# One-hot rows of the expert spread: compare and multiply in one instruction per token

## The reference

```
s = einsum('nhid,hikd->nhik', q, sub_keys)
s_top, i_top = top_k(s, 16)
cand = s_top[:, :, 0, :, None] + s_top[:, :, 1, None, :]
cand_idx = i_top[:, :, 0, :, None] * 128 + i_top[:, :, 1, None, :]
best, pos = top_k(cand.reshape(n, 8, 256), 16)
idx = take_along_axis(cand_idx.reshape(n, 8, -1), pos)
w = softmax(best)
act = gelu(einsum('nhkd,nd->nhk', take(u_tab, idx), hb))
out = einsum('nhk,nhkd->nd', w * act, take(v_tab, idx))
```

## Time and profile before

| | |
|---|---|
| median of 3 runs | 2853.62 us (2851.63 to 2854.61) |
| profiled execution | 2853.46 us, span 2851.7 us |
| mean granted TensorE clock | 0.988 |
| TensorE busy | 2768.9 us (97%) |
| VectorE busy | 1917.7 us (67%) |
| ScalarE busy | 1030.1 us (36%) |
| GpSimd busy | 608.7 us (21%) |

### The profile page before, as it was taken

One profiled execution on the slowest core, in us unless ns is written; L12 is line 12 of the kernel. 1 busy time (PEld: TensorE's weight loads), 2 busy tenths in 40 slices (PEclk: granted clock), 3 DMA queues, 4 the chain that ended last, 5 costly groups with the idle time before them and its releaser, 6 DMA issues. The chain is left out here.

```text
span 2851.7 us, 42463 instructions
## 1 busy us (share of the span) xinstructions
PE 2768.9 (97%) x15946; PEld 2469.1 (87%) x15946; DVE 1917.7 (67%) x3204; ACT 1030.1 (36%) x1502; POOL 608.7 (21%) x432
## 2 busy tenths in 40 slices
PE   8999999999999999999999999999999999899998
PEld 7886778898787898999998999999998777688877
DVE  7666553444445589899966677877777654588843
ACT  6433342223333343344443333333334433322222
POOL 4332000000000166565553322222220000100000
PEclk9999999999999999999999999999999999999999
DMA  3111222201332367888899999999996211232332
GB/s 128 49 56 46 76 94 82 82 29 67 96 96 97 95 216 241 274 288 283 274 298 345 372 318 343 340 342 343 341 341 223 67 45 61 66 100 92 94 89 76
DMA packets 271094, 496.68 MB, mean 174 GB/s; under 512 B 119249, under 2 KB 176721, under 8 KB 270178
## 3 DMA queue, kind: packets, MB, share of 16 engines
q1 hardware_dynamic: 215650, 335.26, 36.4%
q0 software_dynamic: 36864, 134.23, 12.7%
q10 hardware_dynamic: 18432, 25.17, 2.4%
HBM read 442.17 MB, written 52.43 MB: 173 GB/s over the span
## 5 line engine op out<-in xcount | busy, mean ns | idle before, releaser
L283 PE MATMUL banks<-experts_third,weights_high 128*128 128x384 f32 x1024 | 346.0, 338 | 1.0 <-DVE experts_third L2313 1.0
L284 PE MATMUL banks<-experts_third,weights_high 128*128 128x384 f32 x1024 | 345.9, 338 | 0.0
L285 PE MATMUL banks<-experts_third,weights_low 128*128 128x384 f32 x1024 | 345.9, 338 | 0.0
L2086 ACT ACTIVATE weights_high<-weights_raw 128x1024 fp32r<-128x1024 f32 x128 | 135.9, 1062 | 346.7 <-PE banks L285 346.7
L283 PE MATMUL banks<-hn_high,weights_high 128*128 128x264 f32 (+1 forms) x736 | 254.7, 346 | 4.2 <-DVEq L2672 1.7
L2127 POOL TENSOR_TENSOR weights_low<-weights_raw,weights_high 128x1024 fp32r<-128x1024 f32 x63 | 151.2, 2401 | 488.8 <-ACT weights_high L2029 488.7
L283 PE MATMUL banks<-hb_high,weights_high 128*128 128x384 f32 x688 | 240.9, 350 | 7.6 <-DVE weights_low L2292 5.3
L284 PE MATMUL banks<-hn_low,weights_high 128*128 128x264 f32 (+1 forms) x736 | 246.6, 335 | 0.0
L285 PE MATMUL banks<-hn_high,weights_low 128*128 128x264 f32 (+1 forms) x736 | 246.4, 335 | 0.0
L285 PE MATMUL banks<-hb_high,weights_low 128*128 128x384 f32 x688 | 234.1, 340 | 0.0
L284 PE MATMUL banks<-hb_low,weights_high 128*128 128x384 f32 x688 | 234.0, 340 | 0.0
(11 more groups left out here) (574 smaller groups left out, 7083.2 us busy)
## 6 DMA issues: line engine op xcount, KB each, us to landing
weights_raw<-in_u SPq DMA_DIRECT2D x128, 512.0 KB, 6.9
weights_raw<-in_v SPq DMA_DIRECT2D x128, 512.0 KB, 5.8
early_experts<-experts_A ACTq DMA_DIRECT2D x128, 192.0 KB, 4.6
expert_weights<-shared SPq DMA_DIRECT2D x48, 512.0 KB, 7.5
shared<-expert_weights SPq DMA_DIRECT2D x128, 192.0 KB, 5.6
shared<-early_experts SPq DMA_DIRECT2D x128, 192.0 KB, 6.2
weights_raw<-in_w_up SPq DMA_DIRECT2D x44, 512.0 KB, 3.4
weights_raw<-in_w_xbc SPq DMA_DIRECT2D x24, 512.0 KB, 3.5
```

The source lines that it names most:

```text
L283: nc.tensor.matmul(to, w[0], x[0], start=start, stop=False)
L284: nc.tensor.matmul(to, w[0], x[1], start=False, stop=False)
L285: return nc.tensor.matmul(to, w[1], x[0], start=False, stop=stop)
L2086: nc.scalar.activation(high[:, r % 2, :], raw[:, r, :], ACT.Copy).then_inc(v_high, 1)
```

## The change

The column half of the one-hot matrices is still made for four tokens at once, now over 512 elements. The row half is made per token by a tensor-scalar instruction: it compares `iota` with the token's row number and multiplies by the token's weight, both scalars read per partition. Its `iota` is the copy among the constants in SBUF. The weights come from `chosen`, which has a third part for them. The semaphore between compare and multiply goes, and TensorE waits for five signals per group instead of one.

```diff
-        chosen = sb("chosen", [P, 2, DENSE])
+        chosen = sb("chosen", [P, 3, DENSE])
...
-        token_weights = B[:, 4, 2 * P:3 * P]
...
-                    pe.wait_ge(hot_done, n + 1)
+                    pe.wait_ge(hot_done, (PER + 1) * (n + 1))
...
-                    nc.scalar.activation(chosen[:, :, dense_of(b)], B[:, 4, 0:2 * P].rearrange("p (a n) -> p a n", a=2), ACT.Copy
+                    nc.scalar.activation(chosen[:, :, dense_of(b)], B[:, 4, 0:3 * P].rearrange("p (a n) -> p a n", a=3), ACT.Copy
...
-                    here = (n * PER) % P
-                    pairs = [P, 2, PER, P]
-                    nc.vector.tensor_tensor(hots[:, n % 2], iota.unsqueeze(1).unsqueeze(1).to_broadcast(pairs),
-                                            chosen[:, :, four].unsqueeze(3).to_broadcast(pairs), ALU.is_equal).then_inc(hot_equal, 1)
-                    dve.wait_ge(hot_equal, n + 1)
-                    nc.vector.tensor_tensor(rws[:, n % 2], rws[:, n % 2],
-                                            token_weights[:, here:here + PER].unsqueeze(2).to_broadcast([P, PER, P]), ALU.mult
-                                            ).then_inc(hot_done, 1)
+                    nc.vector.tensor_tensor(cols[:, n % 2], iota.unsqueeze(1).to_broadcast([P, PER, P]),
+                                            chosen[:, 1, four].unsqueeze(2).to_broadcast([P, PER, P]), ALU.is_equal).then_inc(hot_done, 1)
+                    for i in range(PER):
+                        token = n * PER + i
+                        nc.vector.tensor_scalar(rws[:, n % 2, i, :], k.const("iota"), chosen[:, 0, token:token + 1],
+                                                chosen[:, 2, token:token + 1], ALU.is_equal, ALU.mult).then_inc(hot_done, 1)
```

More of the change, by code:

```diff
@@ L1831, in experts_phase @@
     KEYS_PART = KEYS // STORES
-    (scored, scores_out, steps, passed, exp_need, exp_done, turned, chosen_out, hot_equal, hot_done, spread_done, copied,
+    (scored, scores_out, steps, passed, exp_need, exp_done, turned, chosen_out, hot_done, spread_done, copied,
      u_high, u_low, u_low_tail, u_done, gelu, v_high, v_low, v_done, a_full, a_high, a_low, added,
      row_index, tables, dotted, dot_gelu, row_weight, v_used, sparse_turned) = k.sems(
-        name, "scored scores_out steps passed exp_need exp_done turned chosen_out hot_equal hot_done spread_done copied "
+        name, "scored scores_out steps passed exp_need exp_done turned chosen_out hot_done spread_done copied "
               "u_high u_low u_low_tail u_done gelu v_high v_low v_done a_full a_high a_low added "
```

## The result

| | before | after |
|---|---|---|
| median of 5 runs, us | 2852.79 | 2866.29 |
| lowest and highest, us | 2851.63, 2854.61 | 2865.48, 2867.68 |
| profiled execution, us (span) | 2853.46 (2851.7) | 2866.0 (2864.2) |

The ratio is 1.005 with a 95% interval of 1.004 to 1.0061: the change made the kernel slower by 13.5 us. The direction was forecast and the time lies in the range given (2860 to 2915), but the forecast was +40 us, three times what came.

The account below looks back on a forecast made before the run. TensorE, busy 97%, bounds the kernel, but VectorE sets the spread tiles' interval. Longer intervals +29, lower clock +16 and small terms -5 sum to +40: 2893 us, 1.4% slower, range 2860 to 2915.

Parts of the forecast that it names:

- The stall: Spread tiles: small VectorE instructions wait until GpSimd's subtraction ends; 16 intervals at 10.25 us, +29.0 us.
- The chain of 6.72 us to the subtraction: Spread tile: TensorE's first expansion leads through its third and ScalarE to GpSimd's subtraction 6.72 us later.
- One group: VectorE's one-hot step for four tokens: 0.61 + 4 x 0.27 = 1.69 us against 1.86.
- What is left behind the subtraction: Spread tile: after 9.10 us the waiting small instructions need up to 1.08 us, and TensorE starts 0.07 later.
- the small terms: Spread stage: undisturbed interval -0.5, earlier run ends -1, kept lead -1.6, one small instruction before GpSimd -2; sum -5 us.
- The clock: TensorE after its waits of 2.45 us: two in three bring a 1.2 GHz stretch costing 1.5 us, +16 us.
- the small one ahead: Spread tiles: one small instruction passes before GpSimd's subtraction in about half of the intervals, -2 us.
- The first intervals of four runs: Four short first intervals in runs of spread tiles keep 0.4 us of lead, -1.6 us.
- That all four keep GpSimd out: Spread tiles: VectorE hands the port between small instructions, so all four pass before the subtraction; 2881 us, chance 0.22.
- That all four are through before it comes: Spread tiles: a group's small instructions finish before GpSimd's subtraction; 2845 us, 0.3% faster, chance 0.12.
- The gathers: Spread tiles: row gathers stop the small instructions too, +0.4 us a tile, +9 us; 2902 us, chance 0.12.
- That nothing changes: Spread tiles: stalls fall into VectorE's idle time, so the time stays 2853 us, chance 0.04.

Follow-up runs that it names:

- The kernel with eight small ones: Changed kernel with four more small instructions, whose output nothing reads, ahead of each tile's first group: 2904.34 us, ratio 1.0193 to the kernel before.

## Why the prediction was right in kind and wrong in size

- **The stall: right.** Small instructions that stand still while GpSimd subtracts, in the first group of each tile, in 16 intervals. Putting just one operand of the old multiply into SBUF makes it (+22 us); a bank operand, a short subtraction or another order each take it away, or most of it. The Trainium skill ("SBUF — State Buffer", Who interferes with whom) has the rule that both halves rest on: a two-input operation with both inputs in SBUF, and the tensor-scalar kind, can collide with GpSimd, and one with at most one SBUF input outside the two-port modes doesn't. The multiply's 1.80 and 0.69 us agree.
- **The chain of 6.72 us to the subtraction: right.** From 1111.66 to 1118.38 are 6.72, and VectorE's greater speed did not shorten it.
- **One group: nearly right.** 1.69 us were forecast and about 1.65 measured; a small instruction has a median of 336 ns where 350 were expected, and 0.25 us from start to start where 0.27 were.
- **What is left behind the subtraction: the step that failed.** The prediction had "The rest wait until 6.72 + 2.38 = 9.10, then need up to 4 x 0.27 = 1.08, and TensorE starts 0.07 later": 1.15 us. Measured are 0.65, from 1120.74 to 1121.39. The first small one (1118.18) went through, and the second, started at 1118.43, stood still but ended 0.1 us after the subtraction, with the third starting at its end. So two small ones remain, not four. The 9.73 us are 6.72 + 2.36 + 0.65. The 0.5 us a tile are 8 us over 16 intervals, of which the small terms had taken off 2. The kernel with eight small ones shows the same count: 10.76 - 6.72 - 2.36 = 1.68 us for six.
- **The clock: right as a mechanism, absent in this kernel.** "16 x 2/3 x 1.5 = 16" was priced for waits of 2.45 us. The waits were 1.65 to 1.75, and none of the 16 intervals shows a low clock. Two things made the forecast wait too long. The failed step put 0.5 us into it. And 2.45 was interval less pace, while the rows that it was compared with give the idle time in brackets, which is smaller for the same wait: 9.73 - 7.80 = 1.93 stands beside 1.65 to 1.69 in brackets, 10.76 - 7.80 = 2.96 beside 2.70. Like for like the forecast was, by my estimate from these two pairs, some 2.2 us, beside one row that fell (2.05) and one that did not (2.20). At 2.45 to 2.72 us in brackets it fell behind 9 of 16. The 16 us are the larger part of the error of 26, and they hang on the smaller part: the length of the wait decides between no fall in 16 and 9 in 16. How often a wait of 2.2 us would have brought one, no run shows.
- **The small terms: right in sign.** 5 us were forecast to come back (2 of them the small one ahead); in the spread stage 3.9 came between the runs of tiles and 0.7 in the last interval. The first intervals of four runs did not keep their lead (9.63 to 9.79 us), and the second run's first interval cost 1.9 that were not forecast. The 5 us behind the stage were not forecast, and what moves them is open.
- **The rivals.** That all four keep GpSimd out: no, one passes and GpSimd comes in at the next. That all four are through before it comes: no, the first starts 6.52 us after the tile's expansion and the last would at 6.52 + 3 x 0.25 = 7.3, after 6.72; the order with the dot moved makes this rival true, and its size (2845 forecast, 2841.79 measured) was about right. The gathers: they do touch the small ones, but little, and not in front of the awaited group. Beside a chain of small ones a gather takes 1.02 to 1.07 us instead of 0.95, and in five places four small ones beside nothing but a gather take 1.19 instead of 1.10 (one of them, in the last spread tile but one, stands below this list). The rule of the same page of the Trainium skill (the "DVE blocks DMA" trap), that a two-port VectorE operation locks GpSimd out while it writes descriptors, shows here as 0.1 us at most, and the small ones pay as much in return. That nothing changes: no.

```profile
1502.64 1.19 DVE L2260 TENSOR_SCALAR experts_hots<-consts,experts_chosen 128x128 f32<-128x128 f32 x4
1502.72 1.06 POOL L2108 DMA_INDIRECT shared<-in_u_rows,experts_row_i  x1 [0.30 <-issue]
```

## What to carry to other kernels

Before an instruction of VectorE loses its only bank operand, look what GpSimd does at that moment: here it made a 0.69 us instruction take 1.80 us and a faster form 0.5% slower. When the stall falls on an awaited group, change the order or keep the old form there, and count what is left of it as well, for an engine without idle time carries it to the next tile; 12 of the 18 us that the faster form is worth with GpSimd out of the way were had with a quarter of the groups left as they were, and 8 with one dot product moved. And where a term of the sum depends on the length of a wait, see which step that length comes from, compare it with waits that are measured in the same way, and give the sum without the term as well.

## What the runs showed of the hardware

- Here VectorE did not keep GpSimd out with a chain of back-to-back instructions: the subtraction's record starts 0.05 us ahead of the second small one, and it is this one that waits.
- A stopped instruction ended sooner after the subtraction than it lasts alone: the multiply of 0.69 us after 0.55, the small one of 0.34 us after 0.1. That it has its start-up behind it by then is the likely reading.
- Two scalars per partition instead of two constants cost about 60 ns each over 128 elements, by the difference of two rows: 336 ns against the 218 of L2218 in the earlier trace rows. The same instruction with its input in a bank takes 415 ns.
- 16 waits of TensorE of 1.65 to 1.75 us left the clock at 2.4 GHz each time; behind 9 of 16 waits of 2.45 to 2.72 us there was a stretch at 1.2 GHz.
